# The final norm of the first six token tiles placed between the last products of the feed-forward block before it

## The chip, the cores and the metric

The kernel runs on one core of one Trainium2 chip. The metric is the device time of one execution in microseconds (us); lower is better. Engine names are those of the profile: PE is TensorE (matmuls and transposes), PEld its weight loads, DVE is VectorE, ACT is ScalarE, POOL is GpSimd, and SP is SyncE, which here only starts transfers (SPq).

## The reference

One inference step of a hybrid encoder layer for 1152 tokens (1024 of a prompt, 128 of samples) of width 1024: a half feed-forward block, a token mixer (sparse attention beside a matrix memory), a second half feed-forward block, and a final norm. The parts that the change touches:

```python
def rmsnorm(x, g):
    x32 = x.astype(jnp.float32)
    y = x32 * lax.rsqrt(jnp.mean(x32 * x32, axis=-1, keepdims=True) + EPS)
    return y.astype(x.dtype) * g

def half_ffn(x, g, w_up, w_down):
    a, b = jnp.split(rmsnorm(x, g) @ w_up, 2, axis=-1)
    return x + 0.5 * ((jax.nn.silu(a) * b) @ w_down)
...
        xp = half_ffn(xp, norm_ffn2[l], w_ffn2_up[l], w_ffn2_down[l])
...
    y_prompt = rmsnorm(xp, norm_final)
    y_sample = rmsnorm(xs, norm_final)
```

## The kernel before, in words

The residual lives in on-chip memory turned over, as `xT`: 8 blocks of 128 features on the partitions, 1152 tokens along each. The program is a row of phases (`load_residual`, `ffn`, `project`, `attention`, `output`, `ffn`, `final_norm`). Each phase is one block with its own queue per engine, written by hand and kept in step by semaphores, and at its end all engines meet at a barrier. The queues run in the order in which they are written; nothing reorders them.

`ffn` runs twice: as `f1` (tag of its tiles) near the start and as `f2` near the end. It works in two halves `h` of 576 tokens (HT), each of two quarters of 288 (QT), and in 11 groups `g` of 256 hidden features. A tile is `(h, kind, g)`: kind `a` and `b` are the two up products, `d` the down product. Tiles follow each other as a0 b0 a1 b1 d0 a2 b2 d1 ... a10 b10 d9 d10, first for h = 0, then for h = 1. A tile has 7 or 8 steps, and `s` counts the steps of all tiles. A step `m` of a `d` tile is one feature block of the residual: PE multiplies it for both quarters (12 matmuls of 288 columns, lines 450 to 452: fp32 is made of three products of high and low parts), and DVE adds half of it to `xT` (line 797, 576 columns). PE may run two such steps ahead of DVE, since the results alternate between two pairs of PSUM banks (4, 5 and 6, 7).

In step s, PE issues the products of s; DVE and ACT first take out the results of s (`evict`) and then do what `rest(s)` lists. In the last 16 steps (d9 and d10 of h = 1) `rest` holds the sums of squares for the norm that comes next: ACT squares a block of 576 tokens (`square`, line 658), and DVE adds it to `acc` (`add_square`, line 817), in d9 for half 0 and in d10 for half 1. POOL makes the low parts of the weights (line 719) and of the hidden features (line 727); it is done with both before d10 begins.

`final_norm` is a phase of its own (tiles `z_...`). PE sums `acc` over the partitions for 9 tiles of 128 tokens (line 2848), DVE and ACT make the root of the inverse mean, PE turns the residual back (line 2855, 8 transposes of 128x128 for a token tile, three tiles in flight), DVE scales tiles 0, 2, 3, 5, 6, 8 and multiplies them by the gain in one instruction (line 2886), ACT scales tiles 1, 4, 7 (line 2866) and POOL multiplies those by the gain (line 2873). SP loads the gain and stores each tile when it is ready (lines 2833, 2842). After the `f1` block, `project` begins with the same kind of sums (line 331).

Of the kernel before, what the change touches and what calls it, by code (L numbers as in the profile page):

```python
# [20 lines left out]
ALU = mybir.AluOpType  # L21
# [3 lines left out]
P = 128  # L25
# [421 lines left out]

def product3(nc, out, w_hi, w_lo, x_hi, x_lo, first, final):
# [6 lines left out]
def ffn(nc, ctx, M, K, w_up, w_down, gain, xT, tag, summed):  # L455
# [15 lines left out]

    for tile in TILES:
        at = len(STEPS)
        COMBO[tile], STEP[tile] = len(LAST), at
        LAST += [at + m for m in ((1, 3, 5, 7) if tile[1] == "d" or plain(tile) else range(7))]
        STEPS += [tile + (m,) for m in range(8 if tile[1] == "d" or plain(tile) else 7)]
# [19 lines left out]
    DIAG_AT = STEP[0, "a", 4]  # L496
    APPLY_AT = {EDGE + e: x for e, x in ((1, "A0"), (2, "B0"), (3, "A1"), (5, "B1"), (8, "A2"), (9, "B2"), (12, "A3"), (13, "B3"))}
    LOW_AT = {EDGE + e: x for e, x in ((3, "A0"), (4, "B0"), (6, "A1"), (7, "B1"), (10, "A2"), (11, "B2"), (14, "A3"), (15, "B3"))}
    S_AT, SL_AT = [(0, 2, 4, 6), tuple(EDGE + e for e in (16, 18, 20, 22))], [(7, 9, 11, 13), tuple(EDGE + e for e in (19, 21, 23, 25))]
    with ExitStack() as mem, M.scope():  # L500
# [4 lines left out]
        xs_hi = M.low(tag + "xs_hi", [P, 8, 4, QT], F32R)  # L505
        xs_lo = M.low(tag + "xs_lo", [P, 8, 4, QT], F32R)
        h_hi = M.low(tag + "h_hi", [P, 2, FG, HT], F32R)
# [9 lines left out]
        sq = M.at(tag + "sq", [P, 2, HT], ev_at)  # L517
# [7 lines left out]
                        [ps[:, 4:6, 0:QT], ps[:, 2:4, 0:QT]], None if summed else ps[:, 0, 0:NT])  # L525
# [65 lines left out]
        with nc.Block() as block:  # L591
            @block.sync
            def _(sp):
                for n, (h, kind, g) in enumerate(TILES):
# [7 lines left out]
                    else:  # L602
                        at = 2 * g * P + (D_FF if kind == "b" else 0)
                        sp.dma_start(dst.rearrange("p (k n) -> p k n", k=KT), up_v[:, :, at:at + 2 * P])\
                            .then_inc(w_in[n % RAWS], 16)

            @block.scalar
            def _(act):
# [37 lines left out]
                def square(h, k):  # L646

                    n = KT * h + k
                    m = (KT - 1) * h + k - 1
                    tok = slice(h * HT, (h + 1) * HT)  # L650
                    act.wait_ge(dn_ev, 8 * (NG * (h + 1) - 1) + k + 1)
                    if k == 0:
                        act.wait_ge(norm.sl_ok, 8)
                    elif m >= 2:
                        act.wait_ge(sum_ok, m - 1)
                    else:
                        act.wait_ge(hm_ok, 4 * 2 * NG)
                    nc.scalar.activation(sq[:, m % 2] if k else K["acc"][:, tok], xT[:, k, tok], ACT.Square)\
                        .then_inc(sq_ok, 1)
# [18 lines left out]
                def rest(s):  # L678
# [30 lines left out]
                for s, step in enumerate(STEPS):  # L709
                    evict(s, *step)  # L710
                    if s in FREED:
                        split_hi(FREED[s])
                    rest(s)

            @block.gpsimd
            def _(pool):
# [23 lines left out]
                for s, step in enumerate(STEPS):  # L740
                    if s in FREED:
                        split_lo(FREED[s])
                    rest(s)

            @block.vector
            def _(dve):
# [41 lines left out]
                def evict(s, h, kind, g, m):  # L788
                    G = group(h, g)
                    if kind == "d":  # L790
                        dve.wait_ge(mm_ok, s + 1)
                        b = 4 + m % 2 * 2
                        x = xT[:, m, h * HT:(h + 1) * HT].rearrange("p (i n) -> p i n", i=2)
# [3 lines left out]
                        v.scalar_tensor_tensor(x, ps[:, b:b + 2, 0:QT], 0.5, x, ALU.mult, ALU.add).then_inc(dn_ev, 1)  # L797
# [10 lines left out]
                def add_square(h, k):  # L808

                    n = KT * h + k  # L810
                    m = (KT - 1) * h + k - 1
                    a = K["acc"][:, h * HT:(h + 1) * HT]
                    if k:
                        dve.wait_ge(sq_ok, n + 1)
                        if m:
                            dve.wait_ge(sum_ok, m)
                        v.tensor_tensor(a, a, sq[:, m % 2], ALU.add).then_inc(sum_ok, 1)

                def rest(s):
# [41 lines left out]
                add_square(1, KT - 1)  # L861

            @block.tensor
            def _(pe):
# [39 lines left out]
                def down(s, h, g, m):  # L904
                    G = group(h, g)
                    j = COMBO[h, "d", g] + m // 2
# [3 lines left out]
                    if 8 * G + m >= 2:  # L910
                        pe.wait_ge(dn_ev, 8 * G + m - 1)
                    hi, lo = slot(w_hi, j), slot(w_lo, j)
                    cols = slice(m % 2 * P, (m % 2 + 1) * P)
                    for i in range(2):
                        out = ps[:, 4 + m % 2 * 2 + i, 0:QT]
# [5 lines left out]

                norm.sums(pe)
                norm.spread(pe, 0)
                for s, (h, kind, g, m) in enumerate(STEPS):
                    if s == EDGE + 1:
# [6 lines left out]
                    else:  # L932
                        up(s, h, kind, g, m)

# [1868 lines left out]
def final_norm(nc, ctx, M, K, io, out, xT):  # L2803


    sem = lambda n: ctx.enter_context(nc.semaphore("z_" + n))
    ON_SCALAR = [t for t in range(NT) if t % 3 == 1]
    with ExitStack() as mem, M.scope():
        gain = M.low("z_gain", [P, D_MODEL])
        part = M.low("z_part", [P, len(ON_SCALAR), D_MODEL])  # L2810
        res = M.low("z_res", [P, NT, D_MODEL])
        ss, inv, rms = (M.low("z_" + n, [P, NT]) for n in ("ss", "inv", "rms"))
        ps = psum(nc, mem, "z_ps", [P, 3, D_MODEL])
        ps_s = psum(nc, mem, "z_ps_s", [P, NT, 1])
        ld, sums, tp, s1, s2, s3, part_ok, r_v, r_g, st = (
            sem(n) for n in ("ld", "sums", "tp", "s1", "s2", "s3", "part_ok", "r_v", "r_g", "st"))

        def results(t):

            g = sum(x <= t for x in ON_SCALAR)  # L2820
            return t + 1 - g, g

        def wait_out(eng, t):

            if t in ON_SCALAR:
                eng.wait_ge(part_ok, results(t)[1])
            else:
                eng.wait_ge(r_v, results(t)[0])

        with nc.Block() as block:  # L2830
            @block.sync
            def _(sp):
                sp.dma_start(gain[:], io["norm_final"].rearrange("(a n) -> a n", a=1).to_broadcast([P, D_MODEL]))\
                    .then_inc(ld, 16)
                for t in range(NT):
                    if t in ON_SCALAR:
                        sp.wait_ge(r_g, results(t)[1])
                    else:
                        sp.wait_ge(r_v, results(t)[0])
                    dst = out["y_prompt"][0, t * P:(t + 1) * P, :] if t < NTP else \  # L2840
                        out["y_sample"].rearrange("b q d -> (b q) d")
                    sp.dma_start(dst, res[:, t]).then_inc(st, 16)
                sp.wait_ge(st, 16 * NT)

            @block.tensor
            def _(pe):
                for t in range(NT):
                    last = nc.tensor.matmul(ps_s[:, t, :], K["acc"][:, t * P:(t + 1) * P], K["ones"][:, 0:1],  # L2848
                                            start=True, stop=True)
                last.then_inc(sums, 1)  # L2850
                for t in range(NT):
                    if t >= 3:
                        wait_out(pe, t - 3)
                    for k in range(KT):
# [140 lines left out]
```

## Time and profile before

| what | value |
|---|---|
| time, median of 3 runs | 2637.28 us (2635.5 to 2637.68) |
| profiled execution: its time | 2635.49 us |
| profiled execution: its span | 2633.7 us |
| PE busy | 2550.8 us, 97% of the span |
| DVE, ACT, POOL busy | 63%, 42%, 57% |
| mean granted TensorE clock | 0.98 of full speed |

The span is the time from the first to the last instruction of the program that the profiler saw; 1.8 us of the execution lie outside it. All times in rows count from the span's start. In rows of instructions, "x8" after an instruction is a count, the two numbers ahead are start and length in us, and square brackets hold the idle time of the engine before it and who ended it. A clock of 1.00 is 2.4 GHz and 0.50 is 1.2 GHz.

### The profile page before, as it was taken

Reading aid. Unit: us, or ns where it says so; the run is one execution under the profiler, and the core shown is the slowest. Engines: PE = TensorE matmul, PEld = TensorE weight load, DVE = VectorE, ACT = ScalarE, POOL = GpSimd, SP = SyncE. Lnnn points to the kernel's source line nnn. Section 1 sums busy time; section 2 is a strip of 40 time slices with the busy share of each in tenths; the row PEclk is TensorE's granted clock in tenths of the full one; section 3 lists DMA queues with packets and bytes.
Section 4 is the critical chain, followed back from the end, with each engine's and each line's share of the span. In section 5 each row is a group of like instructions: output and inputs, shape, how many; then the busy total and the mean of one; then the engine's idle time right before and its main releaser. Section 6 shows DMA issues by size and latency. Waiting matters only on the chain. (4 is left out here: it accounts for less than half of the span.)

```text
span 2633.7 us, 46787 instructions
## 1 busy us (share of the span) xinstructions
PE 2550.8 (97%) x17516; PEld 2480.7 (94%) x17516; DVE 1659.9 (63%) x2925; ACT 1106.6 (42%) x2130; POOL 1502.9 (57%) x1110
## 2 busy tenths in 40 slices
PE   7999999999998999999998998998999999999998
PEld 6999999999997989999987787998999999999998
DVE  8676668666656238998735642425776667666665
ACT  5444444444444332213547763313444444444443
POOL 3988886888885111212223103413888886888884
PEclk8999999999998999999998999998999999999998
DMA  4322222222214212113323303422222222322222
GB/s 153 97 97 97 81 89 89 81 97 97 97 65 137 62 52 77 50 50 103 100 80 79 63 16 119 137 88 80 82 84 92 97 82 96 97 81 92 86 97 81
DMA packets 214944, 230.36 MB, mean 87 GB/s; under 512 B 35196, under 2 KB 192952, under 8 KB 214592
## 3 DMA queue, kind: packets, MB, share of 16 engines
q1 hardware_dynamic: 214720, 227.37, 27.7%
q8 instruction: 141, 2.31, 0.4%
q14 instruction: 83, 0.68, 0.1%
HBM read 200.14 MB, written 25.99 MB: 86 GB/s over the span
## 5 line engine op out<-in xcount | busy, mean ns | idle before, releaser
L719 POOL TENSOR_TENSOR f2w_lo<-f2raw,f2w_hi 128x512 fp32r<-128x512 f32 x224 | 324.7, 1449 | 96.0 <-ACT f2w_hi L616 84.9
L450 PE MATMUL f1ps<-f1xs_lo,f1w_hi 128*128 128x288 f32 x1248 | 371.5, 298 | 6.9 <-DVE f1xs_lo L444 5.5
L450 PE MATMUL f2ps<-f2xs_lo,f2w_hi 128*128 128x288 f32 x1248 | 371.3, 298 | 6.7 <-DVE f2xs_lo L444 4.3
L719 POOL TENSOR_TENSOR f1w_lo<-f1raw,f1w_hi 128x512 fp32r<-128x512 f32 x224 | 325.4, 1453 | 88.1 <-ACT f1w_hi L616 77.3
L451 PE MATMUL f1ps<-f1xs_hi,f1w_lo 128*128 128x288 f32 x1248 | 369.5, 296 | 0.0
L451 PE MATMUL f2ps<-f2xs_hi,f2w_lo 128*128 128x288 f32 x1248 | 369.2, 296 | 0.0
L452 PE MATMUL f1ps<-f1xs_hi,f1w_hi 128*128 128x288 f32 x1248 | 368.3, 295 | 0.0
L452 PE MATMUL f2ps<-f2xs_hi,f2w_hi 128*128 128x288 f32 x1248 | 368.0, 295 | 0.0
L1365 POOL TENSOR_TENSOR d_w_lo<-d_raw,d_w_hi 128x1024 fp32r<-128x1024 f32 x36 | 86.9, 2414 | 414.8 <-ACT d_w_hi L1230 414.7
L450 PE MATMUL d_ps<-xn_lo,d_w_hi 128*128 128x384 f32 x864 | 298.4, 345 | 6.8 <-POOL xn_lo L297 5.2
L451 PE MATMUL d_ps<-xn_hi,d_w_lo 128*128 128x384 f32 x864 | 293.5, 340 | 0.0
L452 PE MATMUL d_ps<-xn_hi,d_w_hi 128*128 128x384 f32 x864 | 293.3, 339 | 0.0
L719 POOL TENSOR_TENSOR f1w_lo<-f1ts,f1w_hi 128x512 fp32r<-128x512 f32 x160 | 231.9, 1449 | 73.7 <-ACT f1w_hi L616 66.2
L719 POOL TENSOR_TENSOR f2w_lo<-f2ts,f2w_hi 128x512 fp32r<-128x512 f32 x160 | 230.8, 1442 | 74.7 <-ACT f2w_hi L616 67.1
L450 PEld LDWEIGHTS f1ps<-f1xs_lo,f1w_hi 128*128 128x128 f32 x1248 | 235.1, 188 | 9.2 <-POOL f1w_lo L719 4.3
L450 PEld LDWEIGHTS f2ps<-f2xs_lo,f2w_hi 128*128 128x128 f32 x1248 | 234.8, 188 | 9.0 <-issue 6.5
L452 PEld LDWEIGHTS f1ps<-f1xs_hi,f1w_hi 128*128 128x128 f32 x1248 | 236.4, 189 | 0.0
L452 PEld LDWEIGHTS f2ps<-f2xs_hi,f2w_hi 128*128 128x128 f32 x1248 | 236.1, 189 | 0.0
L451 PEld LDWEIGHTS f1ps<-f1xs_hi,f1w_lo 128*128 128x128 f32 x1248 | 235.7, 189 | 0.0
L451 PEld LDWEIGHTS f2ps<-f2xs_hi,f2w_lo 128*128 128x128 f32 x1248 | 235.4, 189 | 0.0
L773 DVE TENSOR_TENSOR f1ev<-f1ev,f1ps 128x288 f32<-128x288 f32 x280 | 123.3, 452 | 140.3 <-PE f1ps L452 134.9
L773 DVE TENSOR_TENSOR f2ev<-f2ev,f2ps 128x288 f32<-128x288 f32 x280 | 123.3, 452 | 140.2 <-PE f2ps L452 134.8
(382 smaller groups left out, 6776.9 us busy)
## 6 DMA issues: line engine op xcount, KB each, us to landing
f1raw<-in_w_ffn_up SPq DMA_DIRECT2D x44, 1024.0 KB, 5.1
f2raw<-in_w_ffn_up SPq DMA_DIRECT2D x44, 1024.0 KB, 5.1
f1raw<-in_w_ffn_down SPq DMA_DIRECT2D x22, 1024.0 KB, 4.8
f2raw<-in_w_ffn_down SPq DMA_DIRECT2D x22, 1024.0 KB, 4.9
d_raw<-in_w_in SPq DMA_DIRECT2D x35, 512.0 KB, 5.1
p_dram<-stage SPq DMA_DIRECT2D x24, 576.0 KB, 3.4
b_sg<-p_dram SPq DMA_DIRECT2D x16, 576.0 KB, 4.9
x_dram<-xT SPq DMA_DIRECT2D x1, 4608.0 KB, 15.6
```

The lines of the kernel that those rows point to most:

```text
L450: nc.tensor.matmul(out, w_hi, x_lo, start=first, stop=False)
L451: nc.tensor.matmul(out, w_lo, x_hi, start=False, stop=False)
L452: return nc.tensor.matmul(out, w_hi, x_hi, start=False, stop=final)
L719: nc.gpsimd.tensor_tensor(slot(w_lo, j), source(j), slot(w_hi, j).bitcast(F32), ALU.subtract)\
L773: v.tensor_tensor(ev[:, b + dst], ev[:, b + src], bank(s), ALU.add).then_inc(ad_ok, 1)
L1365: nc.gpsimd.tensor_tensor(w_lo[:, n0 % 2], raw[:, n0 % 2], w_hi[:, n0 % 2].bitcast(F32), ALU.subtract).then_inc(lo_ok, 1)
```

## The change

`final_norm` is no longer a phase. Its work is a class `FinalNorm` whose pieces are called from the step loops of `ffn`, in the second call alone (`last_io`). In the last tile d10 of h = 1 (`FINAL`) the order is by quarters: 16 steps of 6 matmuls, first the 8 feature blocks for tokens 576 to 863, then the 8 for tokens 864 to 1151, and PE may run four steps ahead of DVE instead of two pairs. The sums of squares of half 0 move to the steps from a4 of h = 1 on (`SQUARES_AT`), one block every second step, and those of half 1 go by quarters in d10; this and the quarters hold for both calls of `ffn`. `TAIL` is the first step of d9 of h = 1, and `END` the first of d10.

```diff
+class FinalNorm:
+    PARTS = ((0, 4), (4, 6), (6, 9))
+    SUMS_IN = (2, 2, 7)
+    BY_SCALAR = (1, 3, 4, 7)
+    BY_VECTOR = (0, 2, 5, 6, 7, 8)
...
+    def turn(self, pe, t):
+
+        if 2 <= t < 8:
+            if t - 2 in self.BY_SCALAR:
+                pe.wait_ge(self.part_ok, self.BY_SCALAR.index(t - 2) + 1)
+            else:
+                pe.wait_ge(self.r_v, self.BY_VECTOR.index(t - 2) + 1)
+        x = self.part_of(t)
+        if t % 2 and x < 2:
+            pe.wait_ge(self.mean_ok, x + 1)
...
+    SQUARES_AT = STEP[1, "a", 4]
+    TAIL, END = STEP[1, "d", NG - 2], STEP[FINAL]
...
-        sq = M.at(tag + "sq", [P, 2, HT], ev_at)
+        sq = M.at(tag + "sq", [P, 2, HT], ta1_at)
...
+                if last_io is not None:
+                    sp.wait_ge(mm_ok, TAIL)
+                    z.load(sp)
+                    z.store(sp)
...
-                    if s >= len(STEPS) - 16:
-                        x = s - (len(STEPS) - 16)
-                        square(x // 8, x % 8)
+                    if 0 <= s - SQUARES_AT < 2 * KT and (s - SQUARES_AT) % 2 == 0:
+                        square(0, (s - SQUARES_AT) // 2)
+                    if s >= END:
+                        square(1, s - END)
+                    if last_io is not None:
+                        if s == TAIL + 3:
+                            z.root(act, 0)
+                        if s in (TAIL + 5, END):
+                            z.scaled(act, 1 if s < END else 3)
+                        if s == END + 12:
+                            z.root(act, 1)
+                        if s == END + 13:
+                            z.scaled(act, 4)
...
-                    x = s - (len(STEPS) - 16)
-                    if x > 0:
-                        add_square((x - 1) // 8, (x - 1) % 8)
+                    if 0 < s - SQUARES_AT <= 2 * KT and (s - SQUARES_AT) % 2:
+                        add_square(0, (s - SQUARES_AT) // 2)
+                    if s > END:
+                        add_square(1, s - END - 1)
+                    if last_io is not None:
+                        if s in (TAIL + 2, END + 11):
+                            z.stats(dve, int(s > END))
+                        if s in (TAIL + 4, TAIL + 7, END + 15):
+                            z.result(dve, {TAIL + 4: 0, TAIL + 7: 2, END + 15: 5}[s])
...
-                add_square(1, KT - 1)
+                add_square(1, 2 * KT - 1)
+                if last_io is not None:
+                    z.stats(dve, 2)
+                    for t in (6, 7, 8):
+                        z.result(dve, t)
...
+                    if final:
+                        pe.wait_ge(dn_ev, 8 * G + (m - 3 if m >= 4 else m // 2 - 1))
+                    elif 8 * G + m >= 2:
...
+                def final_norm(s):
+
+                    if s == TAIL + 1:
+                        pe.wait_ge(ad_ok, added(2 * NG - 1, "b", 7))
+                        pe.wait_ge(sum_ok, KT - 1)
+                        z.sums(pe, 0)
+                    if s in (TAIL + 2, TAIL + 4, TAIL + 6, END):
+                        z.turn(pe, (TAIL + 2, TAIL + 4, TAIL + 6, END).index(s))
+                    if s == END + 11:
+                        pe.wait_ge(sum_ok, 2 * (KT - 1))
+                        pe.wait_ge(z.part_ok, 2)
+                        z.sums(pe, 1)
+                    if s in (END + 12, END + 14):
+                        pe.wait_ge(dn_ev, 8 * (2 * NG - 1) + KT)
+                        z.turn(pe, 4 if s == END + 12 else 5)
...
+                if last_io is not None:
+                    pe.wait_ge(dn_ev, 8 * 2 * NG + KT)
+                    z.turn(pe, 6)
+                    pe.wait_ge(sum_ok, 3 * (KT - 1))
+                    z.sums(pe, 2)
+                    z.turn(pe, 7)
+                    z.turn(pe, 8)
```

The methods not shown hold the instructions of the old phase: `sums` one matmul per tile, `stats` the mean and its inverse, `root` the square root, `result` the one instruction of DVE (or, for tile 7, for its right half), `scaled` that of ACT, `gained` that of POOL (for tile 7 for the left half), `load` and `store` those of SP. POOL's `gained` for tiles 1, 3, 4 stands at steps TAIL + 5, END and END + 13, and for tile 7 at the end. PE's results of the norm use banks 0 to 3, which are free once the up products are out, and bank 7 and the pair 4, 5 for the last sums and tile 8.

On PE, at the end of the program, these rows stood before. The `f2ps` rows are the last products, and a sum is two instructions in the trace but one here.

```order
L450 MATMUL f2ps<-f2h_lo,f2w_hi 128x288
L451 MATMUL f2ps<-f2h_hi,f2w_lo 128x288
L452 MATMUL f2ps<-f2h_hi,f2w_hi 128x288
L591 UNCONDITIONAL_BRANCH
L2845 UNCONDITIONAL_BRANCH
L2848 MATMUL z_ps_s<-ones_sb,acc 128x1 x9
L2855 MATMUL z_ps<-ident_sb,xT_21457 128x128 x72
L2830 UNCONDITIONAL_BRANCH
```

And these stand there now, from the last step but one on: the transposes of tile 5, 12 matmuls of the steps END + 14 and END + 15, and what is behind them.

```order
L517 MATMUL f2ps<-ident_sb,xT_21540 128x128 x8
L564 MATMUL f2ps<-f2h_lo,f2w_hi 128x288
...
L566 MATMUL f2ps<-f2h_hi,f2w_hi 128x288
L517 MATMUL f2ps<-ident_sb,xT_21540 128x128 x8
L501 MATMUL f2ps<-ones_sb,acc 128x1 x3
L517 MATMUL f2ps<-ident_sb,xT_21540 128x128 x16
L714 UNCONDITIONAL_BRANCH
```

Behind the last product, 18 rows of sums and 72 transposes became 3 sums and 24 transposes, and the two branches of the barrier between the phases are gone. The other 6 sums and 48 transposes stand between products.

On DVE, the end of the program read like this before, the last two feature blocks of d10 first.

```order
L797 SCALAR_TENSOR_TENSOR xT_21457<-f2ps,xT_21457 128x576
L817 TENSOR_TENSOR acc<-acc,f2sq 128x576
L797 SCALAR_TENSOR_TENSOR xT_21457<-f2ps,xT_21457 128x576
L817 TENSOR_TENSOR acc<-acc,f2sq 128x576 x2
L591 UNCONDITIONAL_BRANCH
L2875 UNCONDITIONAL_BRANCH
L2878 TENSOR_SCALAR z_ss<-z_ps_s 128x9
L2880 RECIPROCAL z_inv<-z_ss 128x9
L2886 SCALAR_TENSOR_TENSOR z_res<-z_ps,z_rms,z_gain 128x1024 x6
```

It reads like this now, from the last feature block of the last quarter on.

```order
L945 SCALAR_TENSOR_TENSOR xT_21540<-f2ps,xT_21540 128x288
L966 TENSOR_TENSOR acc<-acc,f2sq 128x288
L541 SCALAR_TENSOR_TENSOR z_res<-f2ps,stats,z_gain 128x1024
L966 TENSOR_TENSOR acc<-acc,f2sq 128x288
L525 TENSOR_SCALAR stats<-f2ps 128x3
L528 RECIPROCAL stats<-stats 128x3
L541 SCALAR_TENSOR_TENSOR z_res<-f2ps,stats,z_gain 128x1024
L541 SCALAR_TENSOR_TENSOR z_res<-f2ps,stats,z_gain 128x512
L541 SCALAR_TENSOR_TENSOR z_res<-f2ps,stats,z_gain 128x1024
```

The result of tile 5 stands between the last two additions to `acc`, and three results in place of six follow the last inverse.

## Rows read from the trace of the kernel before

**Rows 1.** The page's first part: busy time, share of the span, instructions.
```profile
PE 2550.8 (97%) x17516; PEld 2480.7 (94%) x17516; DVE 1659.9 (63%) x2925; ACT 1106.6 (42%) x2130; POOL 1502.9 (57%) x1110
```
**Rows 2.** The chain of waits that ended last, from 2540 us on: start, length, what.
```profile
2610.33 3.98 PE z_ps_s L2848 x18
2614.31 7.33 PE z_ps L2855 x40
...
2622.86 2.38 POOL z_res L2873
```
**Rows 3.** Windows of the end: length, busy by engine, clock, DMA share, GB/s.
```profile
2607.70:2609.80 2.10, 0.00 (x0) 0.00 (x0) 1.97 (x3) 0.68 (x1) 0.00 (x0) 1.00 0.00 0
2609.80:2620.20 10.40, 9.87 (x47) 9.90 (x48) 2.51 (x5) 2.61 (x3) 1.02 (x1) 0.51 0.30 103
...
2622.40:2632.20 9.80, 2.72 (x25) 2.48 (x23) 3.76 (x3) 1.50 (x2) 4.72 (x2) 0.91 1.02 405
```
**Rows 4.** Timeline of SP's queue at the end: the gain, then the stores.
```profile
2610.28 0.34 SPq L2833 DMA_DIRECT2D z_gain<-in_norm_final  x1
2617.57 10.75 SPq L2842 DMA_DIRECT2D out_y_prompt<-z_res  x8
2628.37 1.22 SPq L2842 DMA_DIRECT2D out_y_sample<-z_res  x1
```
**Rows 5.** The result tiles `z_res`, by tile: the last line is issue to landing.
```profile
L2886 DVE SCALAR_TENSOR_TENSOR z_res<-z_ps,z_rms,z_gain x6: 1273/1283/1283, 2616.3 to 2625.2; 128x1024 f32<-128x1024 f32 x6
L2873 POOL TENSOR_TENSOR z_res<-z_part,z_gain x3: 2344/2367/2375, 2619.2 to 2625.5; 128x1024 f32<-128x1024 f32 x3
...
DMA to landing us min/median/max: 2.6/3.8/4.9
```
**Rows 6.** Timeline of the end on PE, DVE and ACT.
```profile
2607.40 0.29 PE L452 MATMUL f2ps<-f2h_hi,f2w_hi 128*128 128x288 f32 x1
...
2607.73 0.76 DVE L797 SCALAR_TENSOR_TENSOR xT<-f2ps,xT 128x576 f32<-128x576 f32 x1 [0.17 <-PE f2ps L452]
2608.41 1.61 DVE L817 TENSOR_TENSOR acc<-acc,f2sq 128x576 f32<-128x576 f32 x2
2614.35 0.17 DVE L2878 TENSOR_SCALAR z_ss<-z_ps_s 128x9 f32<-128x9 f32 x1 [4.33 <-PE z_ps_s L2848]
...
2614.80 0.21 ACT L2862 ACTIVATE z_rms<-z_inv 128x9 f32<-128x9 f32 x1 [3.22 <-DVE z_inv L2880]
2617.92 1.11 ACT L2866 ACTIVATE z_part<-z_ps,z_rms 128x1024 f32<-128x1024 f32 x1 [2.91 <-PE z_ps L2855]
```
**Rows 7.** Windows for `z_ps` alone, then for `d_ps_t` alone: PE, PEld, others, clock.
```profile
2614.17:2619.96 5.79, 5.79 (x27) 5.79 (x28) 1.67 (x2) 1.11 (x1) 0.50 0.23 93
2620.16:2624.96 4.80, 4.80 (x46) 4.72 (x44) 4.34 (x4) 1.79 (x2) 1.00 0.54 215
...
819.98:821.20 1.22, 1.22 (x11) 1.22 (x12) 0.00 (x0) 1.00 0.11 18
```
**Rows 8.** Timeline of DVE: two additions of 288 columns without a wait between.
```profile
2579.04 0.82 DVE L773 TENSOR_TENSOR f2ev<-f2ev,f2ps 128x288 f32<-128x288 f32 x2 [1.15 <-PE f2ps L452]
```
**Rows 9.** Timeline around the end of the `f1` block.
```profile
817.04 0.29 PE L452 MATMUL f1ps<-f1h_hi,f1w_hi 128*128 128x288 f32 x1
...
818.05 1.61 DVE L817 TENSOR_TENSOR acc<-acc,f1sq 128x576 f32<-128x576 f32 x2
...
819.98 2.77 PE L331 MATMUL d_ps_t<-ones_sb,acc 128*128 128x1 f32 x18 [2.65 <-PEq L591]
```
**Rows 10.** Windows in `f2`: a4, b4 and two steps of d3 of half 1; its start.
```profile
2348.90:2374.50 25.60, 25.60 (x195) 25.60 (x194) 16.65 (x26) 12.44 (x24) 22.20 (x16) 1.00 0.38 124
...
2210.00:2236.00 26.00, 26.00 (x198) 26.00 (x197) 25.39 (x34) 11.40 (x18) 12.38 (x8) 1.00 0.26 82
```
**Rows 11.** By line: DVE instructions with two SBUF inputs; ns shortest, median, longest.
```profile
L760 DVE TENSOR_TENSOR f2ts<-f2raw x80: 677/1250/1831, 1829.3 to 2561.3; 128x512 f32<-128x512 f32 x80
...
L817 DVE TENSOR_TENSOR acc<-acc,f2sq x14: 739/748/1360, 2587.7 to 2609.3; 128x576 f32<-128x576 f32 x14
```

More of the change, by code:

```diff
@@ L452, in product3, with ffn @@
     return nc.tensor.matmul(out, w_hi, x_hi, start=False, stop=final)
-def ffn(nc, ctx, M, K, w_up, w_down, gain, xT, tag, summed):
+def ffn(nc, ctx, M, K, w_up, w_down, gain, xT, tag, first, last_io=None):
     sem = lambda n: ctx.enter_context(nc.semaphore(tag + n))
@@ L470, in plain @@
         return tile[1] != "d" and tile[2] == 0
+    FINAL = TILES[-1]
     for tile in TILES:
@@ L713, in _ @@
                     rest(s)
+                if last_io is not None:
+                    z.root(act, 2)
+                    z.scaled(act, 7)
             @block.gpsimd
@@ L743, in _ @@
                     rest(s)
+                    if last_io is not None and s in (TAIL + 5, END, END + 13):
+                        z.gained(pool, {TAIL + 5: 1, END: 3, END + 13: 4}[s])
+                if last_io is not None:
+                    z.gained(pool, 7)
             @block.vector
@@ L924, in _ @@
                 for s, (h, kind, g, m) in enumerate(STEPS):
+                    if last_io is not None:
+                        final_norm(s)
                     if s == EDGE + 1:
@@ L2800, in _ @@
                 run(lambda n0: None, unit)
[L2803 to L2854, printed above, removed]
-                        last = nc.tensor.transpose(ps[:, t % 3, k * P:(k + 1) * P], xT[:, k, t * P:(t + 1) * P],
-                                                   K["ident"][:])
-                    last.then_inc(tp, 1)
-            @block.scalar
-            def _(act):
-                act.wait_ge(s2, 1)
-                nc.scalar.activation(rms[:], inv[:], ACT.Sqrt).then_inc(s3, 1)
-                act.wait_ge(s3, 1)
-                for x, t in enumerate(ON_SCALAR):
-                    act.wait_ge(tp, t + 1)
-                    nc.scalar.activation(part[:, x], ps[:, t % 3], ACT.Copy, scale=rms[:, t:t + 1]).then_inc(part_ok, 1)
-            @block.gpsimd
-            def _(pool):
-                pool.wait_ge(ld, 16)
-                for x, t in enumerate(ON_SCALAR):
-                    pool.wait_ge(part_ok, x + 1)
-                    nc.gpsimd.tensor_tensor(res[:, t], part[:, x], gain[:], ALU.mult).then_inc(r_g, 1)
-            @block.vector
-            def _(dve):
-                dve.wait_ge(sums, 1)
-                nc.vector.tensor_scalar(ss[:], ps_s[:, :, 0], 1.0 / D_MODEL, EPS, ALU.mult, ALU.add).then_inc(s1, 1)
-                dve.wait_ge(s1, 1)
-                nc.vector.reciprocal(inv[:], ss[:]).then_inc(s2, 1)
-                dve.wait_ge(s3, 1)
-                dve.wait_ge(ld, 16)
-                for t in range(NT):
-                    if t not in ON_SCALAR:
-                        dve.wait_ge(tp, t + 1)
-                        nc.vector.scalar_tensor_tensor(res[:, t], ps[:, t % 3], rms[:, t:t + 1], gain[:],
-                                                       ALU.mult, ALU.mult).then_inc(r_v, 1)
```

140 lines of the change are left out of this document (112 added, 28 removed).

## The prediction, made before the changed kernel had run

> **What bounds the kernel now.** I read the page first: PE is busy for 97% of the span [rows 1], so outside a few places only PE's own work, or work at which PE waits, sets the time. I then read the chain of waits that ended last. Its end is the final norm: sums, transposes, and POOL's last product, which ends at 2625.2 by the chain's pieces [rows 2]. The windows of the last 26 us show four stretches [rows 3]. From 2607.7 PE stands still, while DVE and ACT finish the squares. From 2609.8 PE runs at a granted clock of 0.51, that is 1.2 GHz, with the sums and half of the transposes. From 2622.4 to 2632.2 the DMA engines are fully used (share 1.02, 405 GB/s): eight of the nine stores of 0.52 MB come faster than they drain. So the end is bound one after another by a wait, by a slow clock, and by stores that all fall together; SP issues them from 2617.6 to 2629.6 [rows 4].
>
> The last product of d10 starts at 2607.40 and ends 0.29 later, at 2607.7 [rows 6]. The span ends at 2633.7. These 26.0 us without a product are what the change can shorten.
>
> **What is taken out behind the last product.** I lay the new end out by time after the last product's end.
>
> - DVE takes the last quarter out and finishes `acc`. An instruction of 288 columns takes 0.45, and the second of two follows after 0.37, since two take 0.82 [rows 8]. The order is the last feature block, an addition, the result of tile 5 (1.28 us [rows 5], or 1.25 in a row), and the last addition: 0.04 + 0.37 + 0.37 + 1.25 + 0.45 = 2.5. The result of tile 5 is on this path and costs 1.25 of it.
> - PE turns tile 6 meanwhile. Then it sums three tiles, 6 instructions. At full clock 11 take 1.22 us, 0.111 each [rows 7]; with 0.15 for the last to come out, this ends at 3.3.
> - From the last sum to the root: before, the sums ended at 2614.31 [rows 2] and the root at 2614.80 + 0.21 = 2615.01 [rows 6], so 0.7. Now 4.0.
> - Three results on DVE: 1.25, a half one, and 1.28. A column costs (0.76 - 0.45) / 288 = 1.08 ns [rows 6, 8], so the half takes 1.28 - 0.55 = 0.73. That ends at 7.3. PE's 16 transposes (1.8 us) are ahead of it. ACT's half of tile 7 takes about half of 1.11 [rows 6] and POOL's half of 2.37 [rows 5]: 4.2 + 0.6 + 1.25 = 6.1, inside.
> - Stores of tiles 6, 7 and 8 are issued at 5.3, 6.2 and 7.3. A lone one lands 2.6 us after issue [rows 5], and each takes 0.524 MB / 405 GB/s = 1.3 us of the DMA engines [rows 3]. Tile 6 lands at 7.9, tile 7 at 9.2, tile 8 at 10.5. Before, the last store was issued at 2628.37 and landings took at most 4.9 [rows 4, 5], which leaves 0.4 to the span's end. So the new end is at 10.9.
>
> Saved behind the last product: 26.0 - 10.9 = 15.1 us.
>
> **What is put ahead of the last product.** PE's own work is moved there, and it counts in full, because PE has no idle time there.
>
> - 48 transposes. At full clock 44 weight loads take 4.80 us, 0.109 each; at half clock 28 take 5.79, 0.207 each [rows 7]. Between products the clock is full, so 5.2 us.
> - Sums of 6 tiles, 12 instructions of 0.111: 1.3 us.
> - The products themselves are as many as before.
> - A new wait: the transposes of tile 2 stand one step behind the result of tile 0 (it frees the banks). DVE needs 0.68 (0.76 less the overlap) for step TAIL + 4 and 1.28 for the result, 2.0 us in all, while PE has one step of 12 products. A step takes 1.6 us: 16 steps fill a window of 25.6 us [rows 10]. PE waits 0.4 us. Behind it stand the products of d9, so it costs 0.4. The waits of the other tiles have two or more steps and I cost them at nothing.
> - The gain's load, the stores of tiles 0 to 5, ACT's scalings and POOL's products lie under d9 and d10, where POOL was idle and no weights are loaded. SP has nothing behind them. ACT's table load moves with its first root and is covered by steps of 1.6 us.
>
> Together 7.0 us.
>
> **The quarters.** In d10 a step has 6 products, 0.80 us, and DVE needs 0.37 + 0.37 = 0.74 for it [rows 8]. It fits by little. DVE enters d10 late by the result of tile 2, but PE may now be three steps (2.4 us) ahead, and the sums and transposes of tiles 4 and 5 give 2.2 us back. I take 0. Without overlap a step costs DVE 0.90, and 15 steps would cost PE up to 1.5 us; that is the upper bound.
>
> **The squares of half 0, moved into a4, b4 and d3.** Seven additions and eight squares per block go under products, in steps where PE is fully busy, DVE for 16.65 of 25.6 us and POOL for 22.2 [rows 10]. An addition took 0.75, but 1.36 beside POOL [rows 11]. Seven make 5.2 to 9.5, so DVE comes to 21.9 to 26.2 of 25.6. What hides it is PE's lead of four banks, three steps or 4.8 us. A few steps earlier DVE is busy for 25.39 of 26.0 us and PE still does not wait [rows 10]. I take 0. If the cover were gone it would be up to 1.36 for each of 14 additions.
>
> The Trainium skill (SBUF — State Buffer, section "SBUF: two separate sides") speaks against this edit: a DVE instruction with two SBUF inputs and a GpSimd instruction that reads SBUF share a port pair as an exclusive lock, held for a whole instruction, and the other one is fully blocked. The trace agrees as far as it goes: a subtraction with two SBUF inputs takes 677 ns at the shortest, 1250 in the median and 1831 at the longest [rows 11].
>
> **The end of the first block.** It has the quarters too. From its last product's end (817.04 + 0.29) to the last addition's end (818.05 + 1.61) it takes 2.33 us [rows 9]. Now it is 0.04 + 0.45 for the last quarter, 0.04 + 0.41 for its square (0.6 of ACT's 0.69 for 576 columns), 0.04 + 0.45 for the addition: 1.4. All of `project` starts 0.9 us earlier.
>
> **The sum.** 15.1 - 7.0 + 0.9 = 9.0 us. The profiled span of 2633.7 becomes 2624.7, and its execution of 2635.49 becomes 2626.5. That execution is 1.8 us below the median of the runs, so against the median I predict 2637.28 - 9.0 = 2628.3 us.
>
> **Rivals.**
>
> 1. *The clock falls in the new end, and the quarters make PE wait.* Before, the clock fell to 1.2 GHz at about 2609.8, two us after PE stopped, and came back only near 2620 [rows 3]. The new end has two short pauses of PE, 0.4 and about 0.9 us, with tile 6's transposes between. If it falls, 6 sums cost 0.6 more and the last transposes finish after DVE wants them: 1.4 us in all. With 1.5 for the quarters and another 1 us of waits at tiles 3 to 5, the gain is 5.1 us: 2632.2, on the border of no change. Against it: pauses this short are rare in the trace and nothing shows their effect.
> 2. *The port pair makes PE wait.* If every moved addition waits as the longest subtraction did (1831 - 677 = 1.15 us more [rows 11]), it takes 1.9; seven make 13.3, DVE needs 30.0 of 25.6 us, 4.4 too much for each block. If PE's lead does not absorb this, 8.7 us are lost and the time is 2637.0: no change. For it: POOL is busy for 87% there. Against it: the median of 1250, and the lead of 4.8 us. The page named above would give this if each lock were met at its start.
> 3. *Slower than before.* One mechanism: in a4 and b4, the moved additions delay DVE's additions of the partial sums on which ACT, then DVE, then PE's banks wait, so that each pushes PE by its whole 1.9 us. Then 14 cost 26.6 and the time is 2654.9. It decides against the change from 0.65 us for each addition (9.0 / 14), and shows as slower by over 0.2% from 1.0 us. Against it speak the window with DVE at 98% without a wait of PE, and PE's count of products, as large there as elsewhere [rows 10].
> 4. *The change only moves the end.* If the stores of tiles 3 to 5 queued ahead of the last ones, the end would be bound by DMA as before. Each store needs 1.3 us and d10 lasts 15; it would need all six stores late, and then the gain is about 3 us: 2634.3.
>
> **How the numbers follow.** Runs of this kernel differ by 2 us, so 0.2%, or 5.3 us, is about what can be told from no change; the borders are 2632.0 and 2642.6. My forecast's case, a gain of 7 to 11.5, has 0.72. A larger gain (a shorter wait for the stores) has 0.04, rival 1 with a gain between 4 and 7 has 0.14, of which 0.09 is still faster, rivals 2 and 4 have 0.06, rival 3 has 0.04. Faster: 0.72 + 0.04 + 0.09 = 0.85; same 0.11; slower 0.04. The range runs from a gain of 12 (2625.3) to one of 4.3 (2633.0).
>
> **What would show each step.** Between TAIL and the last product PE has 48 transposes of 0.11 us and one idle gap near 0.4 us ahead of tile 2. The last product ends at about 2613.8 in the span. The last sums start 2.5 us and the last result ends 7.3 us after it, and the span ends 10.9 us after it. In a4 and b4 of half 1, PE has no idle time. PE's first sum after the first block starts 0.9 us earlier. The prediction is wrong if PE waits inside d10 for more than 2 us, if additions in a4 make PE wait, or if the end after the last product is over 14 us.

## The result, and the profile after

| | median | lowest to highest | runs |
|---|---|---|---|
| before | 2635.41 us | 2633.20 to 2638.01 | 20 |
| after | 2639.47 us | 2636.21 to 2643.28 | 20 |

The ratio is 1.0015, with a 95% interval of 1.0009 to 1.0021. The changed kernel is 4 us slower, which is less than the 0.2% that was named as the bound, and it lies outside the predicted range of 2625.3 to 2633.0. The profiled execution took 2637.1 us (the second shortest of the 20) with a span of 2635.3, so it is 1.6 us above the one of before. The page's first part hardly moved against [rows 1].

```profile
PE 2548.7 (97%) x17516; PEld 2476.6 (94%) x17516; DVE 1677.8 (64%) x2959; ACT 1109.0 (42%) x2149; POOL 1507.0 (57%) x1111
```

A sum over the whole span can't show what happened. A timeline of PE, filtered for brackets (idle time before the row, and who ended it), can. First the d3 tiles of half 1, in the first and then in the second block; then d9 and d10 of the second; then the end of each block.

```profile
584.54 0.29 PE L566 MATMUL f1ps<-f1h_hi,f1w_hi 128*128 128x288 f32 x1
587.56 0.37 PE L564 MATMUL f1ps<-f1h_lo,f1w_hi 128*128 128x288 f32 x1 [2.73 <-DVE xT L945]
...
2375.37 0.29 PE L566 MATMUL f2ps<-f2h_hi,f2w_hi 128*128 128x288 f32 x1
2378.39 0.37 PE L564 MATMUL f2ps<-f2h_lo,f2w_hi 128*128 128x288 f32 x1 [2.73 <-DVE xT L945]
...
2600.50 1.09 PE L517 MATMUL f2ps<-ident_sb,xT 128*128 128x128 f32 x8 [0.45 <-DVE z_res L541]
2612.02 0.37 PE L564 MATMUL f2ps<-f2h_lo,f2w_hi 128*128 128x288 f32 x1 [0.83 <-DVE xT L945]
2615.96 0.60 PE L501 MATMUL f2ps<-ones_sb,acc 128*128 128x1 f32 x4 [0.52 <-DVE acc L966]
...
820.65 0.29 PE L566 MATMUL f1ps<-f1h_hi,f1w_hi 128*128 128x288 f32 x1
822.74 1.47 PE L331 MATMUL d_ps_t<-ones_sb,acc 128*128 128x1 f32 x12 [1.79 <-PEq L714]
...
2622.12 0.29 PE L566 MATMUL f2ps<-f2h_hi,f2w_hi 128*128 128x288 f32 x1
2622.96 1.09 PE L517 MATMUL f2ps<-ident_sb,xT 128*128 128x128 f32 x8 [0.55 <-DVE xT L945]
2626.61 0.83 PE L501 MATMUL f2ps<-ones_sb,acc 128*128 128x1 f32 x6 [2.56 <-DVE acc L966]
2627.30 3.19 PE L517 MATMUL f2ps<-ident_sb,xT 128*128 128x128 f32 x16
```

PE now stops for 2.7 us ahead of the third step of d3 in each block, and again for less in d10. The last product ends at 2622.4; 2613.8 was predicted. The windows (columns as in [rows 3]) are the one that answers to [rows 10], the same length of time behind the stop in the first and in the second block, and the end, which answers to [rows 3].

```profile
2349.80:2375.40 25.60, 25.60 (x195) 25.60 (x193) 22.31 (x30) 16.53 (x32) 21.73 (x14) 1.00 0.38 124
...
587.60:591.00 3.40, 3.40 (x26) 3.40 (x27) 2.54 (x3) 0.00 (x0) 3.19 (x3) 1.00 0.00 0
2378.60:2382.00 3.40, 3.40 (x16) 3.40 (x16) 2.17 (x3) 0.00 (x0) 2.98 (x3) 0.51 0.00 0
...
2624.20:2635.30 11.10, 3.88 (x22) 3.48 (x22) 5.92 (x8) 0.89 (x2) 1.75 (x2) 0.82 0.59 236
```

In the window of a4, b4 and the first two steps of d3 DVE is busy for 22.31 us, where it was 16.65; ACT for 16.53, where it was 12.44. Behind the stop in the second block the clock is at 0.51, that is 1.2 GHz: 16 products in 3.4 us in place of 26, which costs 10 x 0.13 = 1.3 us. From the first product of d3 to the first of the next tile the two blocks take 15.70 and 17.24 us, so by this measure the slow clock costs 1.5; before, both took 12.75. The end is no longer bound by the DMA engines (share 0.59, it was 1.02). It is 12.9 us long, from 2622.4 to 2635.3; 10.9 were predicted.

What makes PE stop in d3 is seen on DVE's timeline. First after:

```profile
2359.72 0.46 DVE L918 TENSOR_TENSOR f2ev<-f2ev,f2ps 128x288 f32<-128x288 f32 x1 [0.78 <-PE f2ps L566]
2360.09 1.08 DVE L966 TENSOR_TENSOR acc<-acc,f2sq 128x576 f32<-128x576 f32 x1
...
2362.80 1.85 DVE L966 TENSOR_TENSOR acc<-acc,f2sq 128x576 f32<-128x576 f32 x1
...
2367.75 1.85 DVE L966 TENSOR_TENSOR acc<-acc,f2sq 128x576 f32<-128x576 f32 x1
...
2372.70 0.75 DVE L966 TENSOR_TENSOR acc<-acc,f2sq 128x576 f32<-128x576 f32 x1
...
2374.84 1.00 DVE L931 TENSOR_TENSOR f2ev<-f2ev 128x288 f32<-128x288 f32 x1
2375.76 1.81 DVE L966 TENSOR_TENSOR acc<-acc,f2sq 128x576 f32<-128x576 f32 x1
2377.50 1.41 DVE L945 SCALAR_TENSOR_TENSOR xT<-f2ps,xT 128x576 f32<-128x576 f32 x2
```

And the same steps in the kernel before, DVE again:

```profile
2371.36 0.46 DVE L773 TENSOR_TENSOR f2ev<-f2ev,f2ps 128x288 f32<-128x288 f32 x1 [0.23 <-PE f2ps L452]
2371.92 0.68 DVE L786 TENSOR_TENSOR f2ev<-f2ev 128x288 f32<-128x288 f32 x1
2372.95 0.76 DVE L797 SCALAR_TENSOR_TENSOR xT<-f2ps,xT 128x576 f32<-128x576 f32 x1 [0.35 <-PE f2ps L452]
```

Before, DVE waited 0.35 us for the first step of d3: it was in time. After, no row behind 2359.72 has a bracket, so it waited for nothing until it reaches that step at 2377.50. PE finished the step's products one step ahead of the last ones before its stop (2375.37 + 0.29 = 2375.7, less a step of 1.6), so at about 2374.1. DVE is 3.4 us late, and PE has only one further step of 1.6 us that it may do meanwhile.

### The profile page after: what moved, and what is told of

Same layout as the page of the kernel before. It is cut to its first block and busy times, and to the rows that moved or that the text cites. A ratio compares the mean times of both kernels' runs of the same rounds, so it can differ in the third digit from the quotient of the medians.

```text
span 2635.3 us, 46906 instructions
## 1 busy us (share of the span) xinstructions
PE 2548.7 (97%) x17516; PEld 2476.6 (94%) x17516; DVE 1677.8 (64%) x2959; ACT 1109.0 (42%) x2149; POOL 1507.0 (57%) x1111
## 5 line engine op out<-in xcount | busy, mean ns | idle before, releaser
L564 PE MATMUL f2ps<-f2h_lo,f2w_hi 128*128 128x288 f32 x704 | 209.3, 297 | 5.6 <-DVE xT L945 5.5
L564 PE MATMUL f1ps<-f1h_lo,f1w_hi 128*128 128x288 f32 x704 | 207.8, 295 | 4.5 <-DVE xT L945 4.5
## 6 DMA issues: line engine op xcount, KB each, us to landing
x_dram<-xT SPq DMA_DIRECT2D x1, 4608.0 KB, 15.1
```

## The experiments

**First block as before.** Only the first block's squares of half 0 go back into d9; the quarters stay in both blocks.

```diff
-    SQUARES_AT = STEP[1, "a", 4]
+    SQUARES = [TAIL + k for k in range(KT)] if first else [STEP[1, "a", 4] + 2 * k for k in range(KT)]
...
-                    if 0 <= s - SQUARES_AT < 2 * KT and (s - SQUARES_AT) % 2 == 0:
-                        square(0, (s - SQUARES_AT) // 2)
+                    if s in SQUARES:
+                        square(0, SQUARES.index(s))
```

DVE's additions follow one step behind (`s - 1 in SQUARES`).

> In the first block alone, the squares and additions of half 0 stand in d9 again, one per step, as before the change; the second block is as changed. Theory A (the seven moved additions make DVE late, and d3 with its lead of two steps lets PE wait): PE's stop of 3.0 us ahead of the third product of d3 in the first block is gone, the one in the second block stays, and the first block's last product ends about 3.2 us earlier than in the changed kernel (820.9); the run is about 3 us faster than the changed kernel, so about 1 us slower than the kernel before. Rival B (it is the order by quarters in d10 of the first block that costs): the stop stays or the block's end does not move by more than 0.5 us.

Measured: 2634.14 us (11 runs) against 2634.31, ratio 1.0000 (0.9991 to 1.0009). In the first block PE's stop in d3 is gone; in the second it is still there:

```profile
2374.37 0.37 PE L564 MATMUL f2ps<-f2h_lo,f2w_hi 128*128 128x288 f32 x1 [2.76 <-DVE xT L945]
```

So the moved squares make the stop, block by block, and the quarters don't. The first block's last product ends 2.7 us earlier than in the changed kernel (818.24 in place of 820.94), where 3.2 had been expected. Between the two ratios lie 0.15%, or 4 us, for a stop of 2.7; the intervals allow both.

**Additions with one SBUF input.** Are the additions long because of POOL? Here the first six of half 0 add to `acc` what lies in PSUM banks 4 and 5 in place of the squares, so the sum is another one. To keep that in order PE waits for the sixth ahead of d3.

```diff
+                        if h == 0 and n < KT - 1:
+                            a = a.rearrange("p (i n) -> p i n", i=2)
+                            v.scalar_tensor_tensor(a, ps[:, 4:6, 0:QT], 0.5, a, ALU.mult, ALU.add).then_inc(sum_ok, 1)
...
+                    if (h, g, m) == (1, 3, 0):
+                        pe.wait_ge(sum_ok, KT - 2)
```

> The additions 1 to 6 of half 0 in both blocks read PSUM banks 4 and 5 and the accumulator in place of the squares and the accumulator: as long an instruction, in the same place, but with one SBUF input instead of two (their sums are not the squares' any more). Addition 7 stays as it is. Theory A (an instruction with two SBUF inputs is held behind POOL's instruction): the six take 0.75 to 0.81 us each in place of 0.75 to 1.85, and PE's stop in d3 shrinks from 3.0 us to under 1. Rival C (DVE has simply too much to do there, with or without POOL): the six take 0.8 us and PE still stops for 2 us or more in each block.

Measured: one run of 2637.07 us. DVE's groups between 2345 and 2380 (busy time, mean ns), first here, L968, and then the same in the changed kernel, L966:

```profile
L968 DVE SCALAR_TENSOR_TENSOR acc<-f2ps,acc 128x576 f32<-128x576 f32 x6 | 4.5, 749 | 0.2 <-ACT f2sq L787 0.2
```

```profile
L966 DVE TENSOR_TENSOR acc<-acc,f2sq 128x576 f32<-128x576 f32 x7 | 9.8, 1406 | 0.0
```

With one SBUF input each takes 749 ns beside the same work of POOL; with two, 1406 in the mean. The Trainium skill (SBUF — State Buffer, section "SBUF: two separate sides") says that a DVE instruction meets POOL's lock if it is in a two-port mode or has two SBUF inputs. These two rows agree. Whether the stop goes away with the length this run can't show directly: PE stopped for 2.30 us at the wait that the experiment itself put in.

```profile
2374.15 0.37 PE L564 MATMUL f2ps<-f2h_lo,f2w_hi 128*128 128x288 f32 x1 [2.30 <-DVE acc L968]
```

But DVE's rows around that stop tell how late it was:

```profile
2373.14 0.74 DVE L968 SCALAR_TENSOR_TENSOR acc<-f2ps,acc 128x576 f32<-128x576 f32 x1
2376.26 0.76 DVE L945 SCALAR_TENSOR_TENSOR xT<-f2ps,xT 128x576 f32<-128x576 f32 x1 [2.37 <-PE f2ps L566]
```

With short additions DVE was through with the sixth at 2373.9, 2.0 us behind PE's last product of b4 (2374.15 - 2.30 = 2371.85). Without the added wait PE would have finished the first step of d3 at about 2373.5, so DVE would have been 0.4 us late where the changed kernel's was 3.4, and PE has a further step of 1.6 us to do. By this estimate the stop would be gone, which speaks against the rival that DVE simply has too much to do there.

**Additions spread out.** In both blocks one square goes into the last step ahead of each up tile from a4 to b7, and its addition into that tile's first step. There are as many additions as in the changed kernel, but one per seven or eight steps and none in a tile's last steps.

```diff
+    SQUARES = [STEP[1, k, g] - 1 for g in range(4, 8) for k in "ab"]
```

> The squares of half 0 stand in the last step ahead of each up tile from a4 to b7 and the additions in the first step of those tiles, where DVE has no partial sum to add: one addition per tile, over four groups, in both blocks. Everything else as changed. Theory A: each addition may still take up to 1.9 us, but DVE is not late any more, PE's stops in d3 go to under 0.3 us in both blocks, the clock stays at full speed there, and the kernel is about 7 us faster than the changed one (3 in the first block, 4.3 in the second with its slow clock), so about 3 us faster than before. Rival D (every addition costs PE its own length wherever it stands): PE's stops add up to as much as before, spread.

Measured: 2629.75 us (11 runs) against 2634.31, ratio 0.9982 (0.9973 to 0.9991). PE has no stop in d3 in either block, and the window of 25.6 us that ends there reads:

```profile
2347.50:2373.10 25.60, 25.60 (x194) 25.60 (x193) 18.21 (x27) 13.60 (x26) 22.01 (x16) 1.00 0.37 124
```

A single addition is still long (the one in this stretch took 1531 ns), and PE does not mind it.

**Which additions count.** Two kernels, in each of which some of the moved additions of both blocks are replaced by an instruction of one column, so that those squares are missing in the sum: the first five of the six in a4 and b4 in the first kernel, and in the second only the sixth, in the last step of b4, directly ahead of d3 (`n == 6` in place of `n < 6`).

```diff
+                        if h == 0 and n < 6:
+                            v.tensor_scalar(a[:, 0:1], a[:, 0:1], 1.0, EPS, ALU.mult, ALU.add).then_inc(sum_ok, 1)
```

> The changed kernel, with the first five moved additions of each half 0 (those in a4 and b4, feature blocks 1 to 5) replaced by an instruction of one column; the one directly ahead of d3 and the one in it stay. The sum of squares is left out for these blocks. If DVE's lateness adds up over a4 and b4, the stop ahead of d3's third step (2.7 us in both blocks) is gone or under 0.5 us, and the span is 5 to 8 us shorter (2627 to 2630). If the addition directly ahead of d3 makes the stop by itself, it is still over 1.5 us in both blocks, and the span is 2632 to 2635.

> The changed kernel, with only the sixth moved addition (feature block 6, directly ahead of d3's first step) replaced by an instruction of one column; its part of the sum of squares is left out. If the lateness adds up, the stop in d3 becomes shorter by about one addition's time, 1.1 to 1.9 us, and 0.8 to 1.7 us of it stay. If the sixth alone makes the stop, it is gone (under 0.3 us) in both blocks.

Measured: 2633.13 and 2632.41 us, one run each. PE's stop in d3 without the first five, first and second block:

```profile
585.47 0.37 PE L564 MATMUL f1ps<-f1h_lo,f1w_hi 128*128 128x288 f32 x1 [0.67 <-DVE xT L945]
...
2374.92 0.37 PE L564 MATMUL f2ps<-f2h_lo,f2w_hi 128*128 128x288 f32 x1 [0.67 <-DVE xT L945]
```

And without the sixth:

```profile
585.32 0.37 PE L564 MATMUL f1ps<-f1h_lo,f1w_hi 128*128 128x288 f32 x1 [1.09 <-DVE xT L945]
...
2375.43 0.37 PE L564 MATMUL f2ps<-f2h_lo,f2w_hi 128*128 128x288 f32 x1 [1.08 <-DVE xT L945]
```

The five are worth 2.73 - 0.67 = 2.06 us, the sixth 2.73 - 1.09 = 1.64. The second kernel came out as the theory of added lateness had it (0.8 to 1.7 us left), the first not quite: 0.67 us remain with the sixth alone, a little more than the 0.5 that it had allowed. So the sixth carries nearly as much as it is long (1.81 us), and the five bring DVE late to it; the span of the first (2631.4) was also above its 2627 to 2630. By these sums the six are worth 3.7 us, 1 us more than the stop.

**POOL's products in four pieces.** At the end of the kernel DVE's additions again stood beside POOL, which now multiplies by the gain while the sums are made. First the changed kernel, DVE and POOL:

```profile
2608.97 2.53 DVE L966 TENSOR_TENSOR acc<-acc,f2sq 128x288 f32<-128x288 f32 x1 [0.46 <-ACT f2sq L787]
...
2622.82 2.18 DVE L966 TENSOR_TENSOR acc<-acc,f2sq 128x288 f32<-128x288 f32 x1
2624.92 1.27 DVE L541 SCALAR_TENSOR_TENSOR z_res<-f2ps,stats,z_gain 128x1024 f32<-128x1024 f32 x1
2626.12 0.44 DVE L966 TENSOR_TENSOR acc<-acc,f2sq 128x288 f32<-128x288 f32 x1
...
2608.78 2.41 POOL L557 TENSOR_TENSOR z_res<-z_part,z_gain 128x1024 f32<-128x1024 f32 x1 [7.91 <-ACT z_part L549]
2622.10 2.58 POOL L557 TENSOR_TENSOR z_res<-z_part,z_gain 128x1024 f32<-128x1024 f32 x1 [10.91 <-ACT z_part L549]
```

An addition of 288 columns takes 0.44 elsewhere. Two of them take 2.53 and 2.18, and both end 0.3 us behind a product of POOL. The experiment cuts these products:

```diff
-        self.nc.gpsimd.tensor_tensor(self.res[:, t, cols], self.part[:, n, cols], self.gain[:, cols], ALU.mult)\
-            .then_inc(self.r_g, 1)
-        pool.wait_ge(self.r_g, n + 1)
+        w = (cols.stop - cols.start) // 4
+        for q in range(4):
+            c = slice(cols.start + q * w, cols.start + (q + 1) * w)
+            self.nc.gpsimd.tensor_tensor(self.res[:, t, c], self.part[:, n, c], self.gain[:, c], ALU.mult)\
+                .then_inc(self.r_g, 1)
+            pool.wait_ge(self.r_g, 4 * n + q + 1)
```

> POOL's products by the gain (tiles 1, 3, 4 and the half of 7) are cut into four instructions of a quarter of the columns each, 0.6 us in place of 2.4. Everything else as changed. Theory A: DVE's additions in d10 that took 2.53 and 2.18 us take at most 1.1; PE's stops ahead of the sixth quarter step (1.1 us from one start to the next) and of the second sums (0.8) shrink to under 0.3 each; the last sums start 2.5 to 3 us after the last product in place of 4.2; from d10's first product to the end it is about 3 us shorter. Rival E (DVE is late in d10 because 0.74 us of work for 0.80 us of products leaves no room after the result of tile 2): the stops stay over 0.7 us each.

Measured: one run of 2635.4 us, span 2633.6 (lines are 3 further down here). DVE and PE at the end:

```profile
2622.25 0.55 DVE L969 TENSOR_TENSOR acc<-acc,f2sq 128x288 f32<-128x288 f32 x1
...
2624.57 0.83 PE L501 MATMUL f2ps<-ones_sb,acc 128*128 128x1 f32 x6 [1.08 <-DVE acc L969]
2625.26 1.94 PE L517 MATMUL f2ps<-ident_sb,xT 128*128 128x128 f32 x16
```

The addition takes 0.55 in place of 2.18, the wait ahead of the last sums is 1.08 in place of 2.56, and the last 16 transposes take 1.94 in place of 3.19: the clock stayed up. The stop of 0.83 in d10 is gone, but the one ahead of the second sums is 0.48 where it was 0.52; under 0.3 had been expected, so POOL doesn't make that one. From d10's first product to the end it took 27.7 us in place of 29.9, 2.2 less where about 3 had been expected. The stops in d3 are as in the changed kernel (2.8 us).

**Both together, and the result of tile 5 moved.** The last two kernels spread the additions and cut POOL's products; one also moves DVE's result of tile 5 behind the last addition.

```diff
-                        if s in (TAIL + 4, TAIL + 7, END + 15):
-                            z.result(dve, {TAIL + 4: 0, TAIL + 7: 2, END + 15: 5}[s])
+                        if s in (TAIL + 4, TAIL + 7):
+                            z.result(dve, {TAIL + 4: 0, TAIL + 7: 2}[s])
...
+                    z.result(dve, 5)
                     z.stats(dve, 2)
```

> e3_light_steps and e4_pool_pieces together, the result of tile 5 still between the last two additions. If the two causes are separate, 2625 to 2628 us (e3's 2629.75 less 2 to 4), the granted clock stays at 1.00 behind the last product, and the span ends about 11 us behind the last product, as the prediction had it. If POOL in pieces only moves DVE's waits to other additions, 2629 to 2630 us.

> The squares of half 0 as in e3_light_steps, POOL's products with the gain in four pieces as in e4_pool_pieces, and DVE's result of tile 5 behind the last addition to acc, ahead of the last mean. If the causes named so far (late DVE at d3, POOL's 2.4 us products that hold DVE's additions in d10 and at the end, the result of tile 5 between the last two additions) are separate and all, the gains add: 9.7 us from e3, 0.8 for the stop in d10, 1.5 for the shorter wait ahead of the last sums, some 1.5 for the clock that then does not fall, and 1.2 for the moved result less what it adds behind: 2624 to 2627 us, no stop in d3, the last sums under 2 us behind the last product's end. If the results' chain on DVE sets the end and not the sums, moving the result of tile 5 brings nothing: the time is that of e6_light_and_pieces, within 1 us.

Measured: without the move 2626.90 us (6 runs) against 2634.64, ratio 0.9972 (0.9960 to 0.9983); with it 2626.93 (7 runs), ratio 0.9970 (0.9959 to 0.9981). Both are some 8 us faster than the kernel before and beat the changed kernel by more. The gains of the spread additions (4.6 us under the kernel before) and of the pieces (3 more) add; the moved result brings nothing, as the second case of its expectation had it. With it the last sums start 1.93 us behind the last product's end (2612.45 + 0.29), without it 2.73 (2615.81 + 0.29 to 2618.83), but the last store is issued 7.6 and 7.8 us behind it: of 0.8 us 0.3 arrives. PE, DVE, POOL and SP with the move:

```profile
2614.67 0.83 PE L501 MATMUL f2ps<-ones_sb,acc 128*128 128x1 f32 x6 [0.28 <-DVE acc L969]
...
2616.43 3.13 DVE L541 SCALAR_TENSOR_TENSOR z_res<-f2ps,stats,z_gain 128x1024 f32<-128x1024 f32 x3 [0.34 <-ACT stats L532]
...
2617.85 2.06 POOL L560 TENSOR_TENSOR z_res<-z_part,z_gain 128x128 f32<-128x128 f32 x4 [1.85 <-ACT z_part L549]
...
2620.31 0.45 SPq L494 DMA_DIRECT2D out_y_sample<-z_res  x1
```

DVE's results end at 2619.56, but tile 7 waits for POOL's four small pieces until 2619.91, and its store stands ahead of the last one in SP's queue. In the changed kernel that half tile took POOL 1.27 us in one piece, here 2.06 in four. That it should stay in one piece is argued from these rows; a kernel with it was not run.

## Why the prediction was wrong

Its own terms against the trace, in us; a plus is a gain:

| term of the prediction | predicted | measured |
|---|---|---|
| behind the last product | +15.1 | +13.1 (26.0 to 12.9), the waits and the slow clock there included |
| 48 transposes and 6 sums put ahead | -6.5 | -7.3: d9 and d10 took 34.73 in place of 25.65, 9.1 more, of which 1.8 are the waits in rows below |
| wait at tile 2 | -0.4 | -0.45 |
| end of the first block | +0.9 | +0.85 (2.65 to 1.80) |
| squares of half 0 moved | 0 | -5.5 of stops, -1.3 of slow clock |
| waits of tiles 3 to 5, the quarters, POOL's products | 0 | -0.83 and -0.52 |

The right-hand column gives -1.9, and the profiled executions differ by -1.6. What the prediction has no term for makes the rest, and nearly cancels. Lost: 0.7 in d3, beyond the stops and the 1.3 (15.70 and 17.24 us for twice 12.75), and 0.65 and 1.16 around the change from half 0 to half 1 in the two blocks, of which 0.40 is a stop of PE at 2215.62. Gained: 0.7 in half 0 of the second block, and 2.1 between the first block's last product and the second block's first sum, which took 986.7 us against 989.6, 2.9 less, of which 0.85 is the change's.

The median's 4 us are 2.4 more than this pair of executions shows. Most of that seems to be the granted clock of the one execution that was profiled; that the other 19 were slower for the same reason is not shown, since they left no trace. Three figures speak for it:

- In the 42.7 us behind the first block's last product its clock was 0.88, and PE came to a certain row of `project`, the transposes of `ikw`, 61.4 us behind that product. In the kernels with spread additions, with these and pieces, and without the first five additions, whose instructions there are the same, the clock was 0.80 and it took 63.0 to 63.1 us; four other experiments had 0.88 and 61.4 to 61.6 us. So at least 1.6 of the 2.1 us gained are not the change's.
- Its end took 12.9 us. In the five experiments that leave the end as it is, it took 14.0 (three times), 13.4 and 12.7; where it took 14.0 the six last sums ran at the slow clock as well, 1.44 us in place of 0.83.
- Its mean granted clock was 0.983. The four of the 20 runs with 0.983 or more took 2636.2 to 2638.4 us, the other 16 took 2638.2 to 2643.3.

The steps of the prediction, one by one:

- **The step that failed** is "What hides it is PE's lead of four banks, three steps or 4.8 us." The size of the additions was nearly right: seven were forecast at 5.2 to 9.5 us and took 9.8. (The 22.3 us of the window hold only five of them.) The cover was not there, and it had been put at nothing lost. The lead that counts is that of the tile which comes next. In d3 the results alternate between two pairs of banks, so PE may be two steps ahead, and DVE came 3.4 us late. The window's average hid it: DVE's last wait in it ended at 2359.7, and five of the six additions ahead of d3 stood in the 18 us behind that. Taking the first five away, or the sixth, shortened the stop from 2.73 us to 0.67 or 1.09; spreading all of them removed it. The two stops with the slow clock cost 6.8 us by the table, 7.4 by the length of d3.
- "A few steps earlier DVE is busy for 25.39 of 26.0 us and PE still does not wait" [rows 10] was a true row and a bad witness. That window holds the last 7.7 us of a `d` tile, in which DVE was still in time (it waited for PE ahead of 2213.15), and then up tiles; it doesn't hold a change from up tiles into a `d` tile, where the lead becomes short. Even there the changed kernel had a stop, 0.40 us at 2215.62, when one of DVE's subtractions (`f2xs_lo`, line 444) took 1.80 us in place of 0.75. No moved addition stands before it in that block, so they don't make it; what does was not tested. It is there in all eight experiments too.
- **Rival 2**, the port pair, was the mechanism. It gave 8.7 us of loss and 2637.0, for 0.06 of the chance together with rival 4. The length was nearer to the middle than to the longest: 1.41 in the mean where 1.9 was its price, so each block stopped for 2.7 in place of 4.4, but the slow clock added to it. That its 2637.0 lies near the measured 2639.5 is partly luck: it has neither the slow clock nor what was lost in d9, d10 and the end.
- "POOL's products lie under d9 and d10, where POOL was idle" is the second failed step. They were hidden for POOL and not for DVE, whose additions they held for 2 us each. The rule of the Trainium skill that the prediction cites had been weighed for a4 alone; the additions of 2.53 and 2.18 us show it at work in the tail too. This is most of the 10.9 that became 12.9: the last sums started 4.2 us behind the last product where 2.5 was predicted, and the slow clock did the rest.
- **Rival 1**, the falling clock, came true in its first half: the last 16 transposes took 3.19 us, 0.2 each. The cause was a wait of 2.56 us and not the two short ones that it spoke of; with waits of 0.55 and 1.08 the clock stayed up. The prediction had found nothing that showed what a short pause does; the nearest case in the trace of before is PE's stop of 1.46 us ahead of 852.10, behind which the clock is at 0.52 for 3.4 us.
- The quarters cost nothing by themselves: in the kernel with pieces d10 has no wait inside its products but at the sums (0.48 us). Landing was 2.6 us at the shortest, as taken. The last result stood 9.4 us behind the last product (2631.8), not 7.3; with POOL's products in pieces 7.4. The end then took 11.8, not 10.9.
- One reading of [rows 2] was wrong without harm: POOL's product that ends at 2625.2 is not its last. The last starts at 2625.5 [rows 5] and ends at 2627.8; no term uses it.
- The idea of the change holds. With the additions spread and POOL's products cut it gives 7.7 us where 9.0 was predicted.

## What to carry to other kernels

When work is moved under an engine that is always busy, don't compare busy time with a window's length; follow the lateness of the helping engine to the next place where the bound engine's lead is shortest, and count it there. Put the moved pieces in the first steps of the phases with the longest lead, one at a time. For each DVE instruction with two SBUF inputs ask what POOL does at that moment, also where POOL's work is itself new and "free", and keep POOL's instructions short beside DVE's critical ones.

## What the runs showed that was not expected

- Two stops of PE of the same length, 2.73 us, in the same place of the two blocks: behind the one the clock stayed at 1.00, behind the other it fell to 0.51 for 3.4 us. In the kernel with additions of one SBUF input, in which the stops are of 2.30, it fell in both. A stop of 1.46 us at the start of `project` brought it in the profile of before (0.52 behind 852.10), and the same stop of 1.47 did not in that of the changed kernel (1.00 behind 854.34). So stops of 1.5 to 2.8 us may or may not bring the slow clock; those of 1.09 or less in d3 and at the end did not in these profiles.
- An addition of 288 columns, 0.44 us by itself, took 2.53 us beside one instruction of POOL of 2.41. POOL's own took 2.58 at most where 2.37 was its time before [rows 5]: DVE bore nearly all of the waiting.
